# Decoder-style chain of FFN and mixer stages on one core: modulation weights scaled by ScalarE instead of GpSimd, with other loads, folds and score products re-ordered

## Chip, cores and metric

One core of one Trainium2 chip runs the whole program in one launch. The metric is the device time of that launch in microseconds (us). The kernel is written with raw engine programs: PE (TensorE, the matrix engine), ACT (ScalarE), DVE (VectorE), POOL (GpSimd) and SP (SyncE, which here issues the weight loads) each run their own list, and semaphores tie them together.

## What is computed

A batch of one, 256 tokens, width D = 1024, feed-forward width 2816, all in fp32. Two blocks follow each other. The first has two layers of FFN, mixer, FFN; its mixers are HGRN2 (a gated linear recurrence) and FOX (attention with forget gates). The second has FFN, a token mixer, FFN, each in a modulated frame whose shift, scale and gate come from one vector c.

```python
def first_block(x, ...):
    for layer in range(2):
        x = x + 0.5 * swiglu(rmsnorm(x, norm_g[layer, 0]), ffn_w_in[layer, 0], ffn_w_out[layer, 0])
        hn = rmsnorm(x, norm_g[layer, 1])
        x = x + (hgrn2_mixer(hn, ...) if layer == 0 else fox_mixer(hn, ...))
        x = x + 0.5 * swiglu(rmsnorm(x, norm_g[layer, 2]), ffn_w_in[layer, 1], ffn_w_out[layer, 1])
    return x

def second_block(x, c, w_ada, b_ada, ...):
    mod = (silu(c) @ w_ada + b_ada).reshape(1, 3, 3, 1024)      # w_ada: 1024 x 9216
    def sublayer(h, i, fn, resid_w):
        u = rms_norm(h, norm_pre[i]) * (1.0 + mod[:, i, 1]) + mod[:, i, 0]
        return h + resid_w * mod[:, i, 2] * rms_norm(fn(u), norm_post[i])
    # i = 0: swiglu (weight 0.5), i = 1: token_mixer (1.0), i = 2: swiglu (0.5)
```

## The kernel before, in words

**Stages.** `plan()` lists 13 stages: ffn, hg_in, hg_out, ffn, ffn, fox_in, fox_out, ffn, ffn, tm_in, branch, tm_out, ffn. The text calls the FFN stages by their norm number: 0, 2, 3, 5, 6 and 8. Every stage works on two tiles of 128 tokens.

**Products.** An fp32 product is made of three fp32r matmuls, hi·hi, hi·lo and lo·hi (`three`, lines 568 to 572; the names in a PE row with line 570, 571 or 572 tell which). So every weight exists twice: SP loads 1 MB (128 partitions x 2048 values, two DMAs of 512 KB) into one of four slots of `raw`; ACT's `split_hi` (line 1300) rounds the slot to `w_hi`; DVE's `split_lo` (line 1835) subtracts to make `w_lo`. The left operands are split in the same way (`actT_hi`, `hT_hi`, line 1417; `hT_lo`, line 1978).

**An FFN stage** has 11 chunks of 256 hidden columns (gate and up side by side). For chunk c PE runs `up(c,0)` and `up(c,1)`, 24 matmuls each with the weights of slots 0 and 1, and `down(c-1)`, 24 with those of slot 2. Between `up` and the next chunk stands the way of the hidden values: ACT's `silu` of the gate (lines 1420 to 1426), DVE's `product` with up (line 1988), `blocks`, a 32x32-block transposition (line 1973), ACT's `to_columns`, four DMAs that gather the blocks into columns (line 1411), the cast to `hT_hi` (`turned_hi`, line 1417) and DVE's `turned_lo` (line 1978). The last chunk uses slot 3 and a shorter way: PE transposes `hidden` itself (`turn_hidden_tile`, line 673), ACT writes the high part and DVE's `last_lo` the low. ACT's order within a chunk is: cast of slot 2, cast of hT, cast of slot 0, silu, cast of slot 1, `to_columns`. DVE's: w_lo of slot 2, hT_lo, w_lo of slot 0, product and transposition, w_lo of slot 1.

**Modulation.** silu(c) @ w_ada is not given to PE. POOL does it beside the FFN stages 2, 3, 5 and 6, in 72 units of 128 columns (`ada_unit`, lines 535 to 548), 18 per stage. A unit is a tile of 128 x 8 x 128 values (512 KB, loaded by POOL's own queue, line 533, into one of two buffers); POOL multiplies it with silu(c) (line 539) and adds the eight rows together in three steps (lines 542, 544, 548). Three units make a fold of 384 columns, which DVE finishes in `fold` (a transposition, line 1997, and a sum, line 2000). There are six folds in each of the four stages, placed after the chunks of the table `FOLD_AT`. The buffers lie in `arena`, one large array whose regions many stages share, so a row that says `arena<-arena` tells its operation by its line.

**Start.** ACT normalises x, turns it and casts slots 0 to 3; then it issues twenty small loads (norm vectors, c, biases, constants, the level masks) on its own queue before it enters the first FFN stage. `vectors()` uses them in chunk 5. `rounded_first` (lines 607 to 624) is PE's first product, one slot at a time; it waits for all of w_lo of slot 0 before its first matmul.

**HGRN.** The scores inside a chunk of tokens are made in eight levels (`score(n)`, line 831; `LEVELS`): level n covers the pairs that lie `LEVELS[n]` apart in a binary tree. Each is 16 matmuls of 128 columns by 64 (two tiles, eight heads; line 850), and DVE picks what belongs to the level with a predicated copy under a mask.

**FOX.** Four groups of four heads: `score(g)`, exponentials on ACT (line 1582), `turn_p(g)`, PE's transpositions of the weights (line 1008), and `weigh(g)`. Between them PE runs `unit(c,t)`, the products of the projection that are still due, as cover. DVE's `scaled(g)` inverts the sums and copies the result out, and `gated` multiplies it with the gate.

## Time and profile before

| | before |
|---|---|
| median of 3 runs | 1626.56 us (1624.83 to 1628.05) |
| the profiled execution | 1630.87 us, span 1629.1 us |
| mean granted TensorE clock | 0.995 of full |
| busy PE / PE weight loads | 98% / 81% of the span |
| busy DVE / ACT / POOL | 71% / 50% / 37% |
| moved by DMA | 337.23 MB, mean 207 GB/s |

A profile shows one execution, 4.3 us above the median of the three timed ones. The busy shares are averages over 13 stages. In the rows below, the idle time in brackets is that of the engine just before the row, with the instruction that released it.

### The profile page before, as it was taken

What the parts mean: (1) busy time and instruction counts of PE and PEld (TensorE: products, weight loads), DVE (VectorE), ACT (ScalarE), POOL (GpSimd) and SP (SyncE); (2) the same over time, 40 slices, a digit from 0 to 9 for tenths busy, and PEclk for the clock granted to TensorE, in tenths of its full rate; (3) what the DMA queues carried; (4) which work ended last, traced back from release to release, by engine and by line L of the source; (5) the groups of instructions that cost most, each with busy time, mean ns of one, the idle gap of its engine ahead of it and who ended that gap; (6) DMA issues with size and microseconds to landing.
All of it is one profiled execution on the core that took longest, in us unless ns stands there. A gap on an engine that the chain in (4) does not pass through costs nothing.

```text
span 1629.1 us, 20897 instructions
## 1 busy us (share of the span) xinstructions
PE 1590.8 (98%) x7517; PEld 1313.4 (81%) x7517; DVE 1152.6 (71%) x1114; ACT 821.4 (50%) x983; POOL 604.7 (37%) x368
## 2 busy tenths in 40 slices
PE   6999999999999999999999999999998999999998
PEld 5888888988888788877877888888886788878887
DVE  5565668777877787857777787688786557875554
ACT  5455563354445544445656444554435576564443
POOL 0000100068993599920008899079991000000000
PEclk9999999999999999999999999999999999999999
DMA  7767753348887688854437888758794444547672
GB/s 249 222 196 220 236 195 114 107 158 261 260 271 249 193 280 260 273 194 158 153 105 218 280 261 266 249 184 274 257 288 139 155 155 156 172 136 232 198 220 87
DMA packets 243133, 337.23 MB, mean 207 GB/s; under 512 B 14792, under 2 KB 180994, under 8 KB 243074
## 3 DMA queue, kind: packets, MB, share of 16 engines
q1 hardware_dynamic: 196256, 281.05, 52.6%
q0 software_dynamic: 10512, 38.54, 7.6%
q10 hardware_dynamic: 36306, 16.86, 4.1%
q8 instruction: 36, 0.59, 0.1%
q14 instruction: 23, 0.19, 0.0%
HBM read 319.62 MB, written 1.05 MB: 197 GB/s over the span
## 4 chain that ended last, share of the span: by engine, by line
PE 70%; POOL 17%; DVE 5%; ACT 3%; DMA 2%; issue 2%; ACTq 0%; SPq 0%; DVEq 0%; POOLq 0%
PE ps L570 20%; PE ps L572 20%; PE ps L571 20%; POOL arena L542 5%; POOL arena L539 4%; POOL arena L544 3%; POOL arena L548 2%; PE ps L616 2%; DVE w_lo L1835 2%; PE ps L850 2%; POOL arena L533 2%; DMA arena<-w_ada_dram 1%; PE ps L624 1%; PE ps L578 1%; ACT w_hi L1300 1%
## 5 line engine op out<-in xcount | busy, mean ns | idle before, releaser
L1835 DVE TENSOR_TENSOR w_lo<-raw,w_hi 128x2048 fp32r<-128x2048 f32 x266 | 683.6, 2581 | 204.5 <-ACT w_hi L1300 204.0
L1300 ACT CAST w_hi<-raw 128x2048 fp32r<-128x2048 f32 x266 | 505.7, 1911 | 308.7 <-PE ps L572 270.7
L570 PE MATMUL ps<-w_hi,actT_hi 128*128 128x512 f32 x1456 | 572.7, 393 | 6.4 <-DVE hidden L1988 2.9
L572 PE MATMUL ps<-w_hi,actT_lo 128*128 128x512 f32 x1456 | 567.6, 390 | 0.0
L571 PE MATMUL ps<-w_lo,actT_hi 128*128 128x512 f32 x1456 | 567.3, 390 | 0.0
L570 PEld LDWEIGHTS ps<-w_hi,actT_hi 128*128 128x128 f32 x1456 | 273.6, 188 | 66.5 <-issue 6.5
L572 PEld LDWEIGHTS ps<-w_hi,actT_lo 128*128 128x128 f32 x1456 | 273.7, 188 | 57.8
L571 PEld LDWEIGHTS ps<-w_lo,actT_hi 128*128 128x128 f32 x1456 | 273.9, 188 | 55.4
L542 POOL TENSOR_TENSOR arena<-arena 128x512 f32<-128x512 f32 x72 | 192.0, 2666 | 5.6
L570 PE MATMUL ps<-w_hi,hT_hi 128*128 128x512 f32 x480 | 189.6, 395 | 1.7 <-DVE hT_lo L1978 1.7
L539 POOL TENSOR_TENSOR arena<-arena,c_silu 128x1024 f32<-128x1024 f32 x72 | 153.1, 2126 | 95.6 <-DVE actT_lo L1863 44.6
L571 PE MATMUL ps<-w_lo,hT_hi 128*128 128x512 f32 x480 | 188.2, 392 | 0.0
L572 PE MATMUL ps<-w_hi,hT_lo 128*128 128x512 f32 x480 | 188.0, 392 | 0.0
L533 POOL DMA_DIRECT2D arena<-w_ada_dram x72 | 66.8, 928 | 308.4 <-PE ps L578 286.0
L1988 DVE TENSOR_TENSOR hidden<-gate,ps 128x256 f32<-128x256 f32 x132 | 77.0, 598 | 61.4 <-ACT gate L1426 50.8
L544 POOL TENSOR_TENSOR arena<-arena 128x256 f32<-128x256 f32 x72 | 107.0, 1487 | 5.7
L570 PEld LDWEIGHTS ps<-w_hi,hT_hi 128*128 128x128 f32 x480 | 91.1, 190 | 22.2 <-DVE hT_lo L1978 3.4
L572 PEld LDWEIGHTS ps<-w_hi,hT_lo 128*128 128x128 f32 x480 | 90.9, 189 | 19.4
L571 PEld LDWEIGHTS ps<-w_lo,hT_hi 128*128 128x128 f32 x480 | 91.1, 190 | 18.6
L1426 ACT ACTIVATE gate<-ps 128x256 f32<-128x256 f32 x66 | 25.3, 384 | 137.7 <-PE ps L572 120.4
L548 POOL TENSOR_TENSOR arena<-arena 128x128 f32<-128x128 f32 x72 | 80.4, 1116 | 14.8 <-DVE ada_fold L2000 9.3
L525 POOL CAST hidden<-arena 128x576 uint8<-128x576 f32 x1 | 2.8, 2782 | 191.6 <-PE ps L673 191.6
(257 smaller groups left out, 1349.9 us busy)
## 6 DMA issues: line engine op xcount, KB each, us to landing
raw<-ffn_w_in_dram SPq DMA_DIRECT2D x176, 512.0 KB, 4.9
raw<-ffn_w_out_dram SPq DMA_DIRECT2D x88, 512.0 KB, 4.4
arena<-w_ada_dram POOLq DMA_DIRECT2D x72, 512.0 KB, 6.3
raw<-ffn_w_gate_dram SPq DMA_DIRECT2D x44, 512.0 KB, 4.1
raw<-ffn_w_up_dram SPq DMA_DIRECT2D x44, 512.0 KB, 5.1
raw<-ffn_w_down_dram SPq DMA_DIRECT2D x44, 512.0 KB, 4.4
raw<-w_in_dram SPq DMA_DIRECT2D x40, 512.0 KB, 4.6
raw<-hg_w_in_dram SPq DMA_DIRECT2D x32, 512.0 KB, 4.9
```

What stands on the lines that cost most here:

```text
L533: nc.gpsimd.dma_start(ada_raw[:, n % 2, :, :], w_ada[:, :, n * ADA_U:(n + 1) * ADA_U]).then_inc(ada_loaded[n % 2], 16)
L539: nc.gpsimd.tensor_tensor(r, r, c_silu[:, :].unsqueeze(2).to_broadcast([P, KD, ADA_U]), ALU.mult)\
L542: nc.gpsimd.tensor_tensor(r[:, 0:4, :], r[:, 0:4, :], r[:, 4:8, :], ALU.add).then_inc(ada_by4, 1)
L544: nc.gpsimd.tensor_tensor(r[:, 0:2, :], r[:, 0:2, :], r[:, 2:4, :], ALU.add).then_inc(ada_by2, 1)
L548: nc.gpsimd.tensor_tensor(ada_acc[j % 2][:, at:at + ADA_U], r[:, 0, :], r[:, 1, :], ALU.add).then_inc(ada_summed, 1)
L570: nc.tensor.matmul(to, hi, whi, start=start, stop=False, skip_group_check=True)
L571: nc.tensor.matmul(to, hi, wlo, start=False, stop=False, skip_group_check=True)
L572: return nc.tensor.matmul(to, lo, whi, start=False, stop=stop, skip_group_check=True)
L616: nc.tensor.matmul(to, actT_hi[:, k, tok], half[:, s, w], start=k == 0 and half is w_hi, stop=False, skip_group_check=True)
L1300: nc.scalar.copy(w_hi[:, s, :], raw[:, s, :]).then_inc(hi_ready[s], 1)
L1835: nc.vector.tensor_tensor(w_lo[:, s, :], raw[:, s, :], w_hi[:, s, :].bitcast(F32), ALU.subtract)\
L1988: nc.vector.tensor_tensor(to, g, u, ALU.mult).then_inc(hidden_ready, 1)
```

## The change

Six things are changed. (1) The multiplication of the modulation's units goes from POOL to ACT: `ada_scale(n)` makes eight activations with silu(c) as a per-partition scale; chunk c of the stages 2, 3, 5 and 6 now carries two units, one between the casts of hT and slot 0, the other after `to_columns`. POOL keeps the three additions and the loads; there are three load buffers. (2) `FOLD_AT` has five chunks, and the sixth fold of a stage stands after the last product. (3) The twenty small loads are issued by POOL. (4) Slot 0 of the first stage is loaded, cast and subtracted in two halves, and PE waits for each half. (5) In HGRN the levels 32 and 64 are made as narrow products of 32x32 and 64x64, of which DVE copies all, with no mask. (6) In FOX, `turn_p(3)` moves into the middle of `unit(7,0)`, `scaled` is taken apart, and the gates of tile 0 are turned earlier.

The diff, its core:

```diff
-FOLD_AT = (2, 3, 5, 6, 8, 9)
+FOLD_AT = (2, 4, 5, 7, 8)
...
-        ada_raw = region(5120, 2, KD, ADA_U)
+        ada_raw = region(5120, 3, KD, ADA_U)
...
+                    if st.norm == 0 and half == 0 and isinstance(c, int) and c == 0:
+                        for part, done in ((slice(0, 2), front_loaded), (slice(2, 4), raw_loaded[0])):
+                            nc.sync.dma_start(to[:, part, 0:FC], w_gate[:, part, 0:FC]).then_inc(done, 16)
+                            nc.sync.dma_start(to[:, part, FC:COLS], w_up[:, part, 0:FC]).then_inc(done, 16)
+                        continue
...
+            pool.wait_ge(actT_ready, 4)
+
+            at = 48
+            for v, n in ((a["norm_pre_2"].rearrange("l i (k p) -> (l i k) p", p=P), 24),
+                         (a["norm_post_2"].rearrange("l i (k p) -> (l i k) p", p=P), 24),
...
+            nc.gpsimd.dma_start(rows_a[at:at + 1, :], a["da_subln_2"]).then_inc(rows_loaded, 16)
+            nc.gpsimd.dma_start(rows_b[0:72, :], a["b_ada_2"].rearrange("l (k p) -> (l k) p", p=P)).then_inc(rows_loaded, 16)
...
+            nc.gpsimd.dma_start(zf_raw[:, :, :], tiled(a["fox_w_in"][0])[:, :, 4 * D:FOX_IN]).then_inc(small_loaded, 16)
+            nc.gpsimd.dma_start(consts[:, P:], a["consts"][:, P:]).then_inc(consts_loaded, 16)
+            nc.gpsimd.dma_start(levels_raw, a["levels"]).then_inc(levels_loaded, 16)
+
...
             pool.wait_ge(hT_turned, 2)
             nc.gpsimd.tensor_copy(levels, levels_raw).then_inc(levels_ready, 1)
...
 
             pool.wait_ge(turned, 4 * (by_name["hg_out"].turned + 1))
             pool.wait_ge(c_ready, 1)
 
             def ada_load(n):
-                nc.gpsimd.dma_start(ada_raw[:, n % 2, :, :], w_ada[:, :, n * ADA_U:(n + 1) * ADA_U]).then_inc(ada_loaded[n % 2], 16)
+                nc.gpsimd.dma_start(ada_raw[:, n % 3, :, :], w_ada[:, :, n * ADA_U:(n + 1) * ADA_U]).then_inc(ada_loaded[n % 3], 16)
...
+                j, r = n // ADA_PER, ada_raw[:, n % 3, :, :]
                 at = (n % ADA_PER) * ADA_U
-                pool.wait_ge(ada_loaded[n % 2], 16 * (n // 2 + 1))
-                nc.gpsimd.tensor_tensor(r, r, c_silu[:, :].unsqueeze(2).to_broadcast([P, KD, ADA_U]), ALU.mult)\
-                    .then_inc(ada_scaled, 1)
                 pool.wait_ge(ada_scaled, n + 1)
-                nc.gpsimd.tensor_tensor(r[:, 0:4, :], r[:, 0:4, :], r[:, 4:8, :], ALU.add).then_inc(ada_by4, 1)
-                pool.wait_ge(ada_by4, n + 1)
-                nc.gpsimd.tensor_tensor(r[:, 0:2, :], r[:, 0:2, :], r[:, 2:4, :], ALU.add).then_inc(ada_by2, 1)
-                pool.wait_ge(ada_by2, n + 1)
+                nc.gpsimd.tensor_tensor(r[:, 0:4, :], r[:, 0:4, :], r[:, 4:8, :], ALU.add).then_inc(ada_halved, 1)
+                pool.wait_ge(ada_halved, 2 * n + 1)
+                nc.gpsimd.tensor_tensor(r[:, 0:2, :], r[:, 0:2, :], r[:, 2:4, :], ALU.add).then_inc(ada_halved, 1)
+                pool.wait_ge(ada_halved, 2 * n + 2)
                 if j >= 2 and n % ADA_PER == 0:
                     pool.wait_ge(ada_folded, j - 1)
                 nc.gpsimd.tensor_tensor(ada_acc[j % 2][:, at:at + ADA_U], r[:, 0, :], r[:, 1, :], ALU.add).then_inc(ada_summed, 1)
...
-                    if n == first + half // 2:
-                        pool.wait_ge(actT_ready, 4 * ((8 if first else 4) + 1))
+                    if n % (half // 2) == 0:
+                        pool.wait_ge(ada_scaled, n + 1)
+                        ada_load(n + 2)
                     ada_unit(n)
-                    if n + 2 < first + half:
-                        ada_load(n + 2)
+                    if n + 3 < first + half and n + 1 != first + half // 2:
+                        ada_load(n + 3)
...
                 tok = slice(t * P, (t + 1) * P)
                 for s in range(2):
                     pe.wait_ge(actT_hi_ready, 4 * st.turned + 2 * t + s + 1)
-                    pe.wait_ge(lo_ready[s], st.filled[s] + 1)
+                    if st.norm == s == t == 0:
+                        pe.wait_ge(front_lo, 1)
+                    else:
+                        pe.wait_ge(lo_ready[s], st.filled[s] + 1)
...
+                        if st.norm == s == t == 0 and kk == 2:
+                            pe.wait_ge(lo_ready[s], st.filled[s] + 1)
                         k, w = 4 * s + kk, slice(kk * COLS, (kk + 1) * COLS)
                         for half in (w_hi, w_lo):
                             nc.tensor.matmul(to, actT_hi[:, k, tok], half[:, s, w], start=k == 0 and half is w_hi, stop=False,
...
+                def narrow(n, t, h):
+
+                    size = LEVELS[n]
+                    beside = P // 2 // size
+                    for block in range(beside):
+                        rows = block * 2 * size + (h % 2) * size
+                        at = block * 2 * size
+                        to = ps[rows:rows + size, level_bank(n, t), (h // 2) * size:(h // 2 + 1) * size]
+                        last = nc.tensor.matmul(to, tile(hg_kT, t, h)[:, at:at + size], tile(hg_Q, t, h)[:, at + size:at + 2 * size],
+                                                start=True, stop=True, skip_group_check=True)
+                    return last
+
...
                                 rhs = tile(hg_qT, t, h)
+                            elif LEVELS[n] >= 32:
+                                last = narrow(n, t, h)
...
                 turn_p(2)
                 unit(6, 1)
                 weigh(2)
-                turn_p(3)
-                unit(7, 0)
...
             def token_mixer(st):
 
@@ -1378,6 +1427,13 @@
                 turn(nxt, 2)
...
 
+            def front():
+
+                act.wait_ge(front_loaded, 32)
+                nc.scalar.copy(w_hi[:, 0, 0:SLOT // 2], raw[:, 0, 0:SLOT // 2]).then_inc(front_hi, 1)
+                act.wait_ge(raw_loaded[0], 32)
...
+                        if t == b == 0 and st is None:
+                            front()
+                        elif t == 0:
                             split_hi(b, nxt.filled[b])
...
@@ -1429,13 +1487,23 @@
...
                 to_columns(0)
-                def middle(c):
+                def ada_scale(n):
+                    act.wait_ge(ada_loaded[n % 3], 16 * (n // 3 + 1))
+                    for k in range(KD):
+                        last = nc.scalar.activation(ada_raw[:, n % 3, k, :], ada_raw[:, n % 3, k, :], ACT.Copy, scale=c_silu[:, k:k + 1])
...
+
+                def middle(c, unit=None):
                     split_hi(2, filled[2] + c - 1)
                     turned_hi(c - 1)
+                    if unit is not None:
+                        ada_scale(unit)
                     split_hi(0, filled[0] + c)
                     silu(c)
                     split_hi(1, filled[1] + c + 1)
                     to_columns(c)
+                    if unit is not None:
+                        ada_scale(unit + 1)
...
+                elif st.norm in FOLD_IN:
+                    for c in range(1, NF - 1):
+                        middle(c, ADA_PER * FOLD_IN[st.norm] + 2 * (c - 1))
...
-
-            at = 48
-            for v, n in ((a["norm_pre_2"].rearrange("l i (k p) -> (l i k) p", p=P), 24),
-                         (a["norm_post_2"].rearrange("l i (k p) -> (l i k) p", p=P), 24),
-                         (a["c_2"].rearrange("b (k p) -> (b k) p", p=P), KD),
-                         (a["hg_lb_logits"].rearrange("l (k p) -> (l k) p", p=P), HG_H), (a["hg_out_norm_g"], 1)):
-                nc.scalar.dma_start(rows_a[at:at + n, :], v).then_inc(rows_loaded, 16)
...
-            nc.scalar.dma_start(zf_raw[:, :, :], tiled(a["fox_w_in"][0])[:, :, 4 * D:FOX_IN]).then_inc(zf_loaded, 16)
-            nc.scalar.dma_start(consts[:, P:], a["consts"][:, P:]).then_inc(consts_loaded, 16)
-            nc.scalar.dma_start(levels_raw, a["levels"]).then_inc(levels_loaded, 16)
...
+            def front():
+
+                for at, hi, lo in ((slice(0, SLOT // 2), front_hi, front_lo), (slice(SLOT // 2, SLOT), hi_ready[0], lo_ready[0])):
+                    dve.wait_ge(hi, 1)
+                    nc.vector.tensor_tensor(w_lo[:, 0, at], raw[:, 0, at], w_hi[:, 0, at].bitcast(F32), ALU.subtract)\
+                        .then_inc(lo, 1)
...
+                if st is None:
+                    front()
+                else:
+                    split_lo(0, nxt.filled[0])
...
                 product(NF - 1, False)
+                if st.norm in FOLD_IN:
+                    fold(FOLD_IN[st.norm] + len(FOLD_AT))
                 last_lo(st, 0)
...
@@ -2089,6 +2153,15 @@
                             to = hg_sc[:, t, :, :].rearrange("p g (n two h) -> p g n two h", two=2, h=h)[:, :, :, 1, :]
                             got = ps[:, level_bank(n, t), :].rearrange("p (g n h) -> p g n h", g=HG_H, h=h)
                             m_all = m.rearrange("p (n h) -> p n h", h=h).unsqueeze(1).to_broadcast([P, HG_H, P // (2 * h), h])
+                        if h >= 32:
+                            for odd in range(2):
+                                for block in range(P // 2 // h):
+                                    at, rows = 2 * h * block, 2 * h * block + h * odd
+                                    last = nc.vector.tensor_copy(hg_sc[at:at + h, t, odd:HG_H:2, at + h:at + 2 * h],
+                                                                 ps[rows:rows + h, level_bank(n, t), 0:HG_H // 2 * h]
+                                                                 .rearrange("p (g n) -> p g n", g=HG_H // 2))
+                            last.then_inc(hg_masked, 1)
+                            continue
                         nc.vector.copy_predicated(to, m_all, got).then_inc(hg_masked, 1)
...
-                def scaled(g):
...
                     rinv = f_rinv.rearrange("p (t g pair odd) -> p g t odd pair", t=2, g=4, odd=2)[:, g]
                     step(nc.vector.reciprocal(rinv, sums))
+
+                def keep_result(g):
...
                 dve.wait_ge(fx_o, 2)
                 step.wait()
                 for t in range(TILES):
                     step.mark(gated(0, t))
                 split_lo(0, nxt.filled[0])
+                inverse_sums(3)
+                gated(1, 0).then_inc(src_ready, 1)
+                keep_result(3)
+                dve.wait_ge(fx_o, 4)
+                turn_gated(0)
                 split_lo(1, nxt.filled[1])
-                scaled(3)
-                dve.wait_ge(fx_o, 4)
-                step.wait()
-                for t in range(TILES):
-                    gated(1, t).then_inc(src_ready, 1)
-                    if t == 0:
-                        turn_gated(0)
+                gated(1, 1).then_inc(src_ready, 1)
```

**ACT, inside the chunks of FFN stages 2, 3, 5 and 6.** Before, one chunk (line 1300 is the cast of a slot, 1417 that of hT, 1422 and 1426 the silu, 1411 `to_columns`):

```order
L1300 CAST w_hi<-raw 128x2048
L1414 ISA
L1417 CAST hT_hi<-arena 128x512
L1297 ISA
L1300 CAST w_hi<-raw 128x2048
L1421 REGISTER_ALU
L1422 ACTIVATE gate<-ps 128x256
L1425 REGISTER_ALU
L1426 ACTIVATE gate<-ps 128x256
L1297 ISA
L1300 CAST w_hi<-raw 128x2048
L1411 DMA arena<-arena 128x1x128 x4
```

Now, one chunk (1349 is the cast of a slot, 1475 that of hT, 1480 and 1484 the silu, 1469 `to_columns`, 1493 `ada_scale`):

```order
L1349 CAST w_hi<-raw 128x2048
L1475 CAST hT_hi<-arena 128x512
L1493 ACTIVATE arena<-arena,c_silu 128x128 x8
L1349 CAST w_hi<-raw 128x2048
L1480 ACTIVATE gate<-ps 128x256
L1484 ACTIVATE gate<-ps 128x256
L1349 CAST w_hi<-raw 128x2048
L1469 DMA arena<-arena 128x1x128 x4
L1493 ACTIVATE arena<-arena,c_silu 128x128 x8
```

The first unit stands ahead of the cast of slot 0, the second ahead of the next chunk's cast of slot 2.

**DVE, at the end of such a stage.** Before (1835 is w_lo, 1978 hT_lo, 1988 the product, 2042 `last_lo`, 1997 and 2000 the fold):

```order
L1835 TENSOR_TENSOR w_lo<-raw,w_hi 128x2048
L1997 STREAM_TRANSPOSE arena<-arena 128x384
L2000 TENSOR_REDUCE ada_fold<-arena 128x12
L1835 TENSOR_TENSOR w_lo<-raw,w_hi 128x2048
L1978 TENSOR_TENSOR hT_lo<-arena,hT_hi 128x512
L1835 TENSOR_TENSOR w_lo<-raw,w_hi 128x2048
L1988 TENSOR_TENSOR hidden<-gate,ps 128x256 x2
L2042 TENSOR_TENSOR hT_last_lo<-ps,hT_last_hi 128x256
```

Now (1887 is w_lo, 2040 hT_lo, 2050 the product, 2106 `last_lo`, 2059 and 2062 the fold):

```order
L1887 TENSOR_TENSOR w_lo<-raw,w_hi 128x2048 x2
L2040 TENSOR_TENSOR hT_lo<-arena,hT_hi 128x512
L1887 TENSOR_TENSOR w_lo<-raw,w_hi 128x2048
L2050 TENSOR_TENSOR hidden<-gate,ps 128x256 x2
L2059 STREAM_TRANSPOSE arena<-arena 128x384
L2062 TENSOR_REDUCE ada_fold<-arena 128x12
L2106 TENSOR_TENSOR hT_last_lo<-ps,hT_last_hi 128x256
```

The fold stood two w_lo ahead of the last product; it stands behind the product now, ahead of `last_lo`.

## Rows read from the trace of the kernel before

**Rows 1.** The page: busy time, share of the span and instructions of each engine.
```profile
PE 1590.8 (98%) x7517; PEld 1313.4 (81%) x7517; DVE 1152.6 (71%) x1114; ACT 821.4 (50%) x983; POOL 604.7 (37%) x368
```
**Rows 2.** Timeline, first stage: start, duration, engine, line, operation, [idle before <-releaser].
```profile
12.10 0.77 PE L616 MATMUL ps<-w_hi,actT_hi 128*128 128x512 f32 x1 [2.73 <-DVE w_lo L1835]
12.90 2.28 DVE L1835 TENSOR_TENSOR w_lo<-raw,w_hi 128x2048 fp32r<-128x2048 f32 x1
...
26.75 1.28 ACT L1422 ACT_TABLE_LOAD   x1 [5.23 <-issue]
29.22 0.47 PE L570 MATMUL ps<-w_hi,actT_hi 128*128 128x512 f32 x1 [2.94 <-DVE hidden L1988]
```
**Rows 3.** Timeline, ends of stages 3 and 6; last row: stage 2, chunk 1.
```profile
705.83 0.58 DVE L1997 STREAM_TRANSPOSE arena<-arena 128x384 f32<-128x384 f32 x1 [8.18 <-POOL arena L548]
712.60 0.66 PE L673 MATMUL ps<-consts_sb,hidden 128*128 128x128 f32 x2 [3.24 <-DVE hidden L1988]
...
1226.51 0.58 DVE L1997 STREAM_TRANSPOSE arena<-arena 128x384 f32<-128x384 f32 x1 [8.38 <-POOL arena L548]
1233.28 0.66 PE L673 MATMUL ps<-consts_sb,hidden 128*128 128x128 f32 x2 [4.84 <-DVE hidden L1988]
...
556.70 0.50 PE L570 MATMUL ps<-w_hi,actT_hi 128*128 128x512 f32 x1 [1.69 <-DVE w_lo L1835]
```
**Rows 4.** Windows: PE, PEld, DVE, ACT, POOL busy us; clock, DMA share, GB/s.
```profile
30.40:33.80 3.40, 3.40 (x10) 2.68 (x9) 2.29 (x1) 0.10 (x1) 0.00 (x0) 0.57 0.22 48
713.10:716.50 3.40, 3.40 (x10) 2.65 (x10) 2.80 (x3) 3.18 (x3) 0.00 (x0) 0.58 1.00 352
1231.90:1238.70 6.80, 5.42 (x16) 4.37 (x17) 5.88 (x6) 3.66 (x4) 0.00 (x0) 0.53 0.87 305
```
**Rows 5.** Timeline, PE in the FOX mixer: `turn_p(3)`.
```profile
832.51 0.66 PE L1008 MATMUL ps<-consts_sb,arena 128*128 128x128 f32 x4 [1.81 <-ACT arena L1582]
```
**Rows 6.** Timeline, POOL: multiplication and first addition of one modulation unit.
```profile
857.95 1.89 POOL L539 TENSOR_TENSOR arena<-arena,c_silu 128x1024 f32<-128x1024 f32 x1 [3.10 <-DMA arena<-w_ada_dram]
859.92 1.29 POOL L542 TENSOR_TENSOR arena<-arena 128x512 f32<-128x512 f32 x1
```
**Rows 7.** Timeline, ACT: eight activations from PSUM (`turn`), one from SBUF (`exps`).
```profile
542.62 2.18 ACT L1319 ACTIVATE actT_hi<-ps,cols 128x128 fp32r<-128x128 f32 x8 [0.40 <-PE ps L578]
...
829.24 0.39 ACT L1582 ACTIVATE arena<-arena,small 128x128 f32<-128x128 f32 x1
```
**Rows 8.** Timeline, stage 2, DVE and ACT through one chunk; last row: next silu.
```profile
608.03 4.40 DVE L1835 TENSOR_TENSOR w_lo<-raw,w_hi 128x2048 fp32r<-128x2048 f32 x1 [1.23 <-ACT w_hi L1300]
608.76 0.38 ACT L1422 ACTIVATE gate<-ps 128x256 f32<-128x256 f32 x1 [0.75 <-PE ps L572]
...
611.76 1.91 ACT L1300 CAST w_hi<-raw 128x2048 fp32r<-128x2048 f32 x1
612.35 1.16 DVE L1988 TENSOR_TENSOR hidden<-gate,ps 128x256 f32<-128x256 f32 x2
613.55 0.71 DVE L1973 STREAM_TRANSPOSE arena<-hidden 128x512 f32<-128x512 f32 x1
614.29 2.52 ACTq L1411 DMA_DIRECT2D arena<-arena  x4
...
625.08 0.39 ACT L1422 ACTIVATE gate<-ps 128x256 f32<-128x256 f32 x1 [0.75 <-PE ps L572]
```
**Rows 9.** Timeline, stage 2: PE begins `up(1,0)`; ACT casts hT of chunk 0.
```profile
549.41 0.39 PE L570 MATMUL ps<-w_hi,actT_hi 128*128 128x512 f32 x1
...
557.32 0.62 ACT L1417 CAST hT_hi<-arena 128x512 fp32r<-128x512 f32 x1 [1.16 <-DMA arena<-arena]
```
**Rows 10.** Timeline: a level's 32 score products; eight narrow products; DVE in HGRN.
```profile
304.68 3.68 PE L850 MATMUL ps<-arena 128*128 128x64 f32 x32
...
1275.64 0.28 PE L789 MATMUL ps<-ada_fold,lb 128*32 128x24 f32 x8
...
313.00 1.23 DVE L2143 COPY arena<-ps 128x1024 f32<-128x1024 f32 x1 [2.65 <-PE ps L858]
```

More of the change, by code:

```diff
@@ L1056, in fox, with turn_gates @@
                 weigh(2)
[L1057 to L1058 removed]
+                unit(7, 0, lambda: turn_p(3))
                 weigh(3)
[L1060 removed]
+                def turn_gates():
+                    pe.wait_ge(fx_o, 4)
+                    turn_tile(by_name["fox_out"], fx_g, 0)
+                unit(7, 1, turn_gates)
             def token_mixer(st):
```

58 lines of the change are left out of this document (32 added, 26 removed).

## The prediction

> **What bounds the kernel now.** I read the page's busy times first: the matrix engine (PE) is busy 1590.8 of 1629.1 us [rows 1], so only its waits and its slow stretches can be won. I then went along PE's timeline for every place where it stood still, and asked the rows before it who was late. The reader should see four kinds of place.
>
> At the start, the first product (12.10) waits for w_lo of slot 0, and the up product of chunk 1 (29.22) waits 2.94 us, because ScalarE (ACT) began its silu table load only at 26.75, after 5.23 us of issuing loads [rows 2]. In the two later modulation stages PE waits 3.24 us (712.60) and 4.84 us (1233.28) for `hidden`; just before, VectorE (DVE) had stood 8.18 and 8.38 us in `fold`, waiting for GpSimd (POOL) [rows 3]. At 556.70 PE waits 1.69 us for a w_lo that POOL had held up. Behind the three long stalls PE's granted clock is at its lower level (1.2 GHz instead of 2.4): windows of 3.4, 3.4 and 6.8 us read 0.57, 0.58 and 0.53 [rows 4]. Half speed costs half of each: 1.7, 1.7 and 3.4 us. Last, the FOX mixer's `turn_p(3)` waits 1.81 us for the exponentials [rows 5].
>
> **The change, part by part.** The sum is made against the profiled execution (1630.87 us, span 1629.1).
>
> *Head.* PE's 12.10 is set by w_lo of the whole slot. With half slots it can start when actT_hi is there, about 1.3 us sooner. But eight products at the slow pitch later it needs w_lo of slot 1, which ends at 15.18 [rows 2] and moves by some 0.3 us only. I count 0.5 us. The twenty small loads leave ACT's queue: the table load comes 5.2 us sooner, so the 2.94 us go, and with them the slow window behind. Sum: -0.5 - 2.9 - 1.7 = **-5.1 us**. POOL issues those loads instead; it was idle, and PE needs the vectors first in chunk 5, five chunks of 16 us later, so I cost this at nothing. If that cover failed, the wait would sit in `turn_vectors`.
>
> *Old modulation stalls.* DVE's two long folds and the contested w_lo go: -(3.24 + 1.7) - (4.84 + 3.4) - 1.69 = **-14.9 us**. POOL's multiplication of 1.89 us per unit goes too; what remains begins with an addition of 1.29 us [rows 6]. POOL is then paced by ACT, two units per chunk.
>
> *New ACT work.* Each chunk gets two units of eight 128x128 activations with a per-partition scale. No row shows that form from SBUF. The nearest: eight such from PSUM take 2.18 us, and one from SBUF with a per-partition bias 0.39 us [rows 7], so eight with no overlap would be 3.1. I take 2.3, near the overlapped row, since ACT's neighbours overlap by about 0.1 us wherever they are queued. A ScalarE page of the Trainium skill ("ScalarE: Activation LUTs", section "What ACT_TABLE_LOAD costs") speaks against the change here: with one pointer operand it gives 280 ns + 0.833 ns per element and an overlap of 93 ns, an estimate of 2.44 us for eight. By it the sum below would be some 6 us higher; the PSUM row is the only measured one, and no run here shows the SBUF form yet.
>
> What is queued behind those units matters more than ACT's load. Follow one chunk round [rows 8]: DVE's transposition of `hidden` 0.71, four DMA issues on ACT 2.52 and a pause of about 0.3, unit B 2.3, cast of slot 2 1.91, cast of hT 0.62, unit A 2.3, cast of slot 0 1.91, w_lo of slot 0 2.29, the two products of `hidden` 1.16, and again the transposition. That is 16.0 us, less some 0.4 for ACT's overlaps, plus what POOL takes from DVE: a w_lo of 2.29 became 4.40 beside POOL, and unit A's additions start just before w_lo of slot 0, so 0.2 to 1.0. The loop is 15.8 to 16.6 us long; PE's chunk is 16.32 (silu to silu, 608.76 to 625.08). So ACT has no time left to catch up.
>
> And it starts late. In chunk 1 the cast of hT ends 8.5 us after PE begins `up(1,0)` (557.94 against 549.41) [rows 9]. Unit A, cast, w_lo, products and transposition put the transposition's end at 8.5 + 2.2 + 1.8 + 2.5 + 1.9 = 16.9, which is 6 us after the end of `up(1,1)` (10.9), where it was 2.8 before. If the loop holds this, the last unit B ends about 10.8 us after `up(9,1)`. Then cast 1.9, w_lo of slot 2 2.3, turned_lo 0.6, w_lo of slot 3 2.3 and the first product 0.6 come one after another, with some port wait: 18.7, while PE wants `hidden` at 16.3. **Each of the four stages ends in a stall of about 2.4 us**, of the same kind as at 712.60, plus about 0.3 in chunk 1 and 0.3 in the others: 4 x 3.0 = **+12.0 us**. A stall of 2.94 us cost a slow window, one of 1.69 none; I give two of the four one: **+3.4 us**. The fold that moves to the stage's end (1.15 us) stands behind the product there and ahead of last_lo, which PE wants 2.7 us later; I cost it at nothing.
>
> *FOX.* `turn_p(3)` moves into the middle of unit (7,0), 2.7 us of matmuls later, and the 1.81 us vanish; 1.5 net, since the transposes lose their clean cover: **-1.5 us**. The reordered gates wait for nothing that is late.
>
> *HGRN scores.* The levels 32 and 64 took 3.68 us of PE each by the row, the last one's tail of some 0.2 included: 32 instructions, 0.11 apart. Now 64 instructions of 32x32 and 32 of 64x64. Eight of 32x24 took 0.28 us, so 0.035 each is the low end, and 0.115 the high [rows 10]: 96 of them between 3.4 and 11.0 us against 7.0, that is from -3.6 to +4.0. I take 0.045 and 0.08 (the smaller form lies near the 32x24 row): 5.5 against 7.0, **-1.5 us**. DVE's eight plus four small copies instead of four predicated ones lengthen it by about a microsecond; it waited 2.65 us for PE just after.
>
> Sum: -5.1 - 14.9 + 12.0 + 3.4 - 1.5 - 1.5 = -7.6, so 1623.3 for that execution. It lay 4.3 us above the median of the runs shown; the forecast against the median is **1619 us**.
>
> **The rivals.** *The loop has room.* If a unit takes about 2.1 us, or POOL rarely meets w_lo of slot 0, the loop is 15.8 and gains half a microsecond per chunk: after nine chunks the 3 us of delay are gone and a stage loses 1.0, with no slow window. -5.1 - 14.9 - 3.0 (FOX and HGRN) + 4.0 = -19.0, that is **1607.6**. For it: eight from PSUM take 2.18. Against it: the late start of the loop, and that the row from SBUF reads 0.39 us for one.
>
> *The loop sets the pace (slower).* In ACT's chain between units B and A, from a unit length of about 2.5 us on, the loop exceeds 16.32 by more than 0.3 and each chunk pays. At 2.7 us and a port wait of 1.0 it is 17.1: 9 x 0.8 + 2.6 + 1.7 = 11.5 per stage, +46 in all against the 23.0 removed elsewhere: +23, about **1649**; at 2.55 us about 6.5 per stage, +26, that is 1630. Against it: 2.7 needs activations that hardly overlap.
>
> *The narrow scores cost.* If small matmuls keep the pitch of 0.11, the change there is +4.0 instead of -1.5: **1624.5**. For it: the pitch was the same for 64 and 128 columns. Against it: the 32x24 row.
>
> *The head gains nothing*, because slot loads become the limit once PE is 5 us earlier: 1624. ACT's casts of those slots were held up by its own issues, not by a load, so I hold it unlikely.
>
> **How the numbers follow.** About 0.2% (3.3 us) is what a measurement of this kernel can tell from no change: faster is under 1623.3, slower over 1629.8. Forecast 0.45, room in the loop 0.30, pace set by the loop 0.13, narrow scores or head failing 0.12. Most of the first and all of the second are faster: 0.72. The upper edge of the first and the last make 0.15 the same, the third 0.13 slower. The range reaches to the second (1606) and into the third (1632).
>
> **What would show it.** PE's waits: none at 29 us; no long fold waits on DVE; at each of the four stages' ends a PE wait of about 2.4 us for `hidden`, with DVE running two w_lo ahead of the product. ACT: eight activations in about 2.3 us, and its cast of slot 2 beginning 10 us after `up` ends, not 5.4. If those stalls are missing, the first rival holds; if PE waits in every chunk for w_lo of slot 2 or `hidden`, the second; if the narrow scores' instructions read above 0.075 us on average, the third. The forecast is wrong if ACT's chain is not what DVE waits for at the stage's end.

## The result and the profile after

The changed kernel takes 1632.83 us (median of 20 runs, 1626.28 to 1637.47), the kernel before 1626.43 (20 runs, 1622.86 to 1628.83). The ratio is 1.0035, 95% interval 1.0023 to 1.0047 (the two medians alone give 1.0039): **slower by 0.35%**, where 1619 was forecast, so faster, with a range up to 1632. The execution profiled after took 1634.08 us, 3.2 more than the one before; their difference stage by stage is the first thing to read. I took the start of each stage from PE's timeline (its first transposition of an activation tile) and compared the lengths; the bracket joins the four stages that carry the modulation, for which the forecast was one sum.

| part | before, us | change, us | forecast |
|---|---|---|---|
| start and FFN 0 | 191.73 | -2.97 | -5.1 |
| HGRN | 127.70 | -3.50 | -1.5 |
| FFN 2 | 187.45 | +6.93 | } |
| FFN 3 | 189.21 | -3.65 | } together |
| FFN 5 | 187.57 | +11.25 | } +0.5 |
| FFN 6 | 196.22 | -2.97 | } |
| FOX | 119.37 | -1.80 | -1.5 |
| all else | | below 0.1 | 0 |

So the loss is in the four stages with the modulation: +11.56 in sum against +0.5. The page's busy times, the line that answers to [rows 1]:

```profile
PE 1592.0 (98%) x7549; PEld 1308.3 (80%) x7549; DVE 1064.2 (65%) x1123; ACT 978.5 (60%) x1560; POOL 399.7 (24%) x315
```

ACT gained 157 us of work, POOL and DVE lost 205 and 88; PE's time is the same. No engine beside PE is busy for more than 65% of the span, and yet the kernel is slower. PE's waits, from its timeline at the ends of stages 2, 3, 5 and 6, with one from the middle of stage 5 (to set beside [rows 3]):

```profile
522.67 0.66 PE L704 MATMUL ps<-consts_sb,hidden 128*128 128x128 f32 x2 [3.73 <-DVE hidden L2050]
710.94 0.41 PE L704 MATMUL ps<-consts_sb,hidden 128*128 128x128 f32 x2 [2.81 <-DVE hidden L2050]
973.53 0.50 PE L596 MATMUL ps<-w_hi,hT_hi 128*128 128x512 f32 x1 [0.58 <-DVE hT_lo L2040]
1045.87 0.66 PE L704 MATMUL ps<-consts_sb,hidden 128*128 128x128 f32 x2 [4.79 <-DVE hidden L2050]
1237.18 0.41 PE L704 MATMUL ps<-consts_sb,hidden 128*128 128x128 f32 x2 [2.28 <-DVE hidden L2050]
```

Each of the four stages ends in the wait that was forecast, for the `hidden` that was forecast, but they sum to 13.6 us and not 9.6. In the middle of stage 5 stand seven waits of 0.20 to 0.58 us, for hT_lo and for `hidden`, where the kernel before has none of the kind. Behind three of the four the clock is low (windows; the columns are those of [rows 4]):

```profile
521.70:528.50 6.80, 5.83 (x16) 4.60 (x17) 6.73 (x8) 4.17 (x6) 0.00 (x0) 0.50 0.48 154
713.50:715.10 1.60, 1.60 (x10) 1.29 (x9) 1.60 (x2) 1.56 (x3) 0.00 (x0) 1.00 0.91 350
1044.00:1050.80 6.80, 4.93 (x13) 3.99 (x14) 6.73 (x8) 5.08 (x6) 0.00 (x0) 0.50 0.49 155
1237.70:1242.80 5.10, 5.10 (x18) 3.95 (x17) 5.03 (x5) 3.58 (x4) 0.00 (x0) 0.67 1.04 390
```

The column behind the five engines is the granted clock: 0.50 is half speed, and 0.67 says that a part of that window ran at half speed. Half of 5.83 and of 4.93, and a third of 5.10 us, are 7.1 us lost to half speed, where I had 3.4.

Now one round of stage 5, from one transposition of `hidden` to the next, 16.99 us later; PE's chunk is 16.32. These are rows of the timelines of DVE, ACT and POOL, to set beside [rows 8]:

```profile
945.15 0.71 DVE L2035 STREAM_TRANSPOSE arena<-hidden 128x512 f32<-128x512 f32 x1
945.52 0.90 POOL L561 DMA_DIRECT2D arena<-w_ada_dram  x1 [0.30 <-POOL arena L573]
945.89 2.54 ACTq L1469 DMA_DIRECT2D arena<-arena  x4
948.48 2.45 ACT L1493 ACTIVATE arena<-arena,c_silu 128x128 f32<-128x128 f32 x8 [4.86 <-issue]
950.84 1.90 ACT L1349 CAST w_hi<-raw 128x2048 fp32r<-128x2048 f32 x1
953.55 0.62 ACT L1475 CAST hT_hi<-arena 128x512 fp32r<-128x512 f32 x1 [0.81 <-DMA arena<-arena]
954.08 2.45 ACT L1493 ACTIVATE arena<-arena,c_silu 128x128 f32<-128x128 f32 x8
956.43 1.90 ACT L1349 CAST w_hi<-raw 128x2048 fp32r<-128x2048 f32 x1
958.36 2.71 DVE L1887 TENSOR_TENSOR w_lo<-raw,w_hi 128x2048 fp32r<-128x2048 f32 x1 [2.21 <-ACT w_hi L1349]
960.99 1.11 DVE L2050 TENSOR_TENSOR hidden<-gate,ps 128x256 f32<-128x256 f32 x2
962.14 0.71 DVE L2035 STREAM_TRANSPOSE arena<-hidden 128x512 f32<-128x512 f32 x1
```

The chain is the one that the prediction followed, with one link that it had as a pause of 0.3: at 952.74 ACT is done with the cast of slot 2 and stands still for 0.81 us until the four gathers of `to_columns` have landed. (A DMA has landed when it signals that it is done; its issue alone takes 0.6 us.) And POOL, whose additions of the first unit have just ended, issues its next load of 512 KB at 945.52, ahead of the gathers at 945.89. In the rows of the page that count DMA issues (KB each, median us to landing) the gathers read, after:

```profile
arena<-arena ACTq DMA_DIRECT2D x240, 64.0 KB, 5.0
```

and before:

```profile
arena<-arena ACTq DMA_DIRECT2D x240, 64.0 KB, 3.7
```

These rows count all six FFN stages. In the four with the modulation alone, the medians are 5.5 after and 4.25 before.

Mean length of rounds 2 to 9 in the four stages: 16.60, 16.49, 17.14 and 16.72 us. When the cast of hT waits for nothing, it begins 7.5 us after the transposition and the round is 16.2 to 16.5 (8 of the 32 rounds); else it begins at 7.7 to 9.5, at worst 10.6, and the round is up to 19.0. The wait for the gathers is 0.47, 0.57, 0.91 and 0.60 us per round in the mean of each stage. When POOL issues its load plays a part already here: in 11 of the 32 rounds the load goes out some 0.45 us ahead of the transposition, and 8 of these casts wait for nothing; in the other 21 it goes out later, between 0.04 us ahead of it and 0.9 us behind it, and every one of these casts waits.

### The profile page after: what moved, and what is told of

The parts are those of the page before. It is cut to its first block, busy times and chain, and to the rows that moved or that the text cites. A ratio compares the mean times of both kernels' runs of the same rounds, so it can differ in the third digit from the quotient of the medians.

```text
span 1632.3 us, 21153 instructions
## 1 busy us (share of the span) xinstructions
PE 1592.0 (98%) x7549; PEld 1308.3 (80%) x7549; DVE 1064.2 (65%) x1123; ACT 978.5 (60%) x1560; POOL 399.7 (24%) x315
## 4 chain that ended last, share of the span: by engine, by line
PE 54%; ACT 15%; DMA 10%; DVE 9%; issue 7%; ACTq 5%; SPq 0%; DVEq 0%
PE ps L596 14%; PE ps L598 14%; PE ps L597 14%; DMA arena<-arena 9%; ACT arena L1493 7%; ACT w_hi L1349 6%; ACTq L1469 5%; PE ps L647 4%; DVE w_lo L1887 3%; DVE hidden L2050 3%; PE ps L655 2%; DVE arena L2035 2%; PE ps L896 1%; PE ps L604 1%; DMA raw<-ffn_w_in_dram 0%
## 5 line engine op out<-in xcount | busy, mean ns | idle before, releaser
L1887 DVE TENSOR_TENSOR w_lo<-raw,w_hi 128x2048 fp32r<-128x2048 f32 x265 | 621.9, 2357 | 348.8 <-ACT w_hi L1349 348.5
L596 PE MATMUL ps<-w_hi,actT_hi 128*128 128x512 f32 x1456 | 572.2, 393 | 2.4 <-DVE w_lo L1887 0.7
L1493 ACT ACTIVATE arena<-arena,c_silu 128x128 f32<-128x128 f32 x576 | 176.5, 389 | 171.9 <-issue 171.9
L567 POOL TENSOR_TENSOR arena<-arena 128x512 f32<-128x512 f32 x72 | 93.5, 1299 | 185.7 <-ACT arena L1493 185.0
L573 POOL TENSOR_TENSOR arena<-arena 128x128 f32<-128x128 f32 x72 | 131.8, 1831 | 5.7
L569 POOL TENSOR_TENSOR arena<-arena 128x256 f32<-128x256 f32 x72 | 94.5, 1312 | 5.6
L647 PE MATMUL ps<-w_hi,actT_hi 128*128 128x512 f32 x144 | 59.3, 412 | 2.8 <-DVE w_lo L1887 1.4
```

The source lines that it names most:

```text
L567: nc.gpsimd.tensor_tensor(r[:, 0:4, :], r[:, 0:4, :], r[:, 4:8, :], ALU.add).then_inc(ada_halved, 1)
L569: nc.gpsimd.tensor_tensor(r[:, 0:2, :], r[:, 0:2, :], r[:, 2:4, :], ALU.add).then_inc(ada_halved, 1)
L573: nc.gpsimd.tensor_tensor(ada_acc[j % 2][:, at:at + ADA_U], r[:, 0, :], r[:, 1, :], ALU.add).then_inc(ada_summed, 1)
L596: nc.tensor.matmul(to, hi, whi, start=start, stop=False, skip_group_check=True)
L647: nc.tensor.matmul(to, actT_hi[:, k, tok], half[:, s, w], start=k == 0 and half is w_hi, stop=False, skip_group_check=True)
L1493: last = nc.scalar.activation(ada_raw[:, n % 3, k, :], ada_raw[:, n % 3, k, :], ACT.Copy, scale=c_silu[:, k:k + 1])
```

## The experiments

Two theories stood at first. *ACT's row* (that of the prediction): the round is the sum of ACT's work on the chain, and both units count alike. *Landing*: the gathers' landing sets the cast of hT, so that only the first unit counts, and what delays the landing is the trouble. A rival to both: the loss is in the other parts of the change, or in their being together.

**e1: everything but the scaling.** The changed kernel with `ada_load`, `ada_unit`, ACT's `middle`, `FOLD_AT` and the place of the sixth fold as before. The core of the edit:

```diff
-                    if unit is not None:
-                        ada_scale(unit)
...
-FOLD_AT = (2, 4, 5, 7, 8)
+FOLD_AT = (2, 3, 5, 6, 8, 9)
```

> The changed kernel with the modulation as before: POOL multiplies, two buffers, six folds inside the loop, no unit on ACT. Kept: small loads on POOL, half slots, narrow scores, FOX order. If the parts add up as the two traces have them (head -3.1, HGRN -3.5, FOX -1.8, the two output stages -1.1 us), it takes 9.5 us less than the kernel before: 1617. If instead the loss of the change sits in one of these four parts, or they don't add, it lies within 3 us of the kernel before.

Measured 1619.18 us, ratio 0.9962 [0.9948, 0.9975]. The four other parts are worth 7 us; the scaling turns this into a loss. The 1617 was 2 us too good.

**e2 and e3: one unit cut down to one activation.**

```diff
-                    for k in range(KD):
+                    for k in range(KD - 1 if n % 2 == 0 else 0, KD):
```

This is e2, the first unit; e3 has `n % 2 == 1`, the second. Both leave seven of that unit's eight rows unscaled.

> The changed kernel, but the first unit of each chunk (between the casts of hT and slot 0) does one of its eight activations, so half of the modulation's rows stay unscaled. Theory landing (the round of a chunk goes transposition, four issues, landing of hT at 8.0 to 8.6 us, cast of hT, first unit, cast of slot 0, w_lo, product): the round falls from 16.2 to 17.0 us by 2.1, below PE's 16.32, and the stalls of all four stages go: 1632.8 - 27 = 1606. Theory of the prediction (ACT's own row of work is the round, both units count alike): the same, 1606. If neither unit matters (POOL's additions or the loads do it): 1630.

> The changed kernel, but the second unit of each chunk (behind to_columns) does one of its eight activations. Theory landing: hT lands at 8.0 to 8.6 us whether or not ACT is busy in between, so the cast of hT keeps its place, the round stays near 16.3 to 16.9 us, and the time stays above 1622. Theory of the prediction: the second unit is a term of the round like the first, the round falls by 2.1, 1606.

e2: 1607.18, ratio 0.9878 [0.9863, 0.9893]. e3: 1608.01, ratio 0.989 [0.9873, 0.9907]. By the times, landing is refuted: the second unit is worth as much as the first. By the traces it isn't. In e3 ACT is free 2 us sooner, and then waits for the gathers 1.6 us longer (2.23 us per round in the mean, against 0.64). ACT's timeline, stage 5:

```profile
939.70 0.62 ACT L1475 CAST hT_hi<-arena 128x512 fp32r<-128x512 f32 x1 [1.68 <-DMA arena<-arena]
```

The cast of hT begins 7.3 us after the transposition there. The median of the 32 rounds is 7.6 us, against 8.3 with the whole unit, and the mean round is 16.25 instead of 16.74. Half a microsecond for 2 us of work taken out: so the landing does hold most of it back. But 16.25 lies below PE's 16.32 and 16.74 above, and with that half microsecond 25 us of the time are gone. My error in this expectation was to take a round that hardly changes for a time that hardly changes. In e2, too, the round fell by 0.5 and not by 2.1 (mean 16.21): w_lo of slot 0 now runs beside POOL's first addition and the start of its second, and takes 4.2 us in this round, 4.0 in the median instead of 2.6 (timelines of DVE and POOL):

```profile
991.66 4.20 DVE L1887 TENSOR_TENSOR w_lo<-raw,w_hi 128x2048 fp32r<-128x2048 f32 x1
992.39 1.30 POOL L567 TENSOR_TENSOR arena<-arena 128x512 f32<-128x512 f32 x1
993.77 2.68 POOL L569 TENSOR_TENSOR arena<-arena 128x256 f32<-128x256 f32 x1
```

**e4: the first unit elsewhere.** All work is done.

```diff
                     turned_hi(c - 1)
-                    if unit is not None:
-                        ada_scale(unit)
                     split_hi(0, filled[0] + c)
                     silu(c)
                     split_hi(1, filled[1] + c + 1)
+                    if unit is not None:
+                        ada_scale(unit)
                     to_columns(c)
```

> The changed kernel with the first unit moved from behind the cast of hT to behind the cast of slot 1, ahead of to_columns, where ACT waits some 2.3 us for DVE's transposition. All work is done. Both theories of the round: the unit leaves it, the round is some 14.5 us, stalls at the four stage ends go, 1606 to 1610. Rival: the unit ends later than the transposition, to_columns comes later by up to 2 us and hT with it; then the stalls stay and the time is 1625 or more.

Measured **1604.73 us** (1604.01 to 1605.31), ratio 0.9868 [0.9853, 0.9883]: faster than both kernels, by 1.3% than the one before. None of the four stage ends has a wait for `hidden` any more, and the rounds read 16.3, PE's own chunk, not the chain's 14.5: a chain shorter than the chunk waits for PE. ACT's timeline shows why the rival failed:

```profile
912.07 0.55 ACTq L1469 DMA_DIRECT2D arena<-arena  x1
912.33 0.69 ACT L1493 ACTIVATE arena<-arena,c_silu 128x128 f32<-128x128 f32 x2
912.65 0.63 ACTq L1469 DMA_DIRECT2D arena<-arena  x1
912.92 0.68 ACT L1493 ACTIVATE arena<-arena,c_silu 128x128 f32<-128x128 f32 x2
...
913.97 0.64 ACTq L1469 DMA_DIRECT2D arena<-arena  x1
914.09 3.02 ACT L1493 ACTIVATE arena<-arena,c_silu 128x128 f32<-128x128 f32 x10
917.02 1.90 ACT L1349 CAST w_hi<-raw 128x2048 fp32r<-128x2048 f32 x1
918.82 0.61 ACT L1475 CAST hT_hi<-arena 128x512 fp32r<-128x512 f32 x1
```

The unit stands ahead of the four issues in the program, and runs beside them: ACT computes while its queue issues. So both units together end 5.7 us after the transposition (911.33), just as one did behind the issues. The loads have moved as well, away from the gathers, whose median is 3.7 us again (4.0 in the four stages). So e4 changes two things at once, the unit's place and the moment of the loads, and doesn't tell their shares.

**e5 and e6: a dose less and a dose more.** e5 does six of the first unit's eight activations (it reads 1.87 instead of 2.45 us); e6 makes two of its rows in halves, ten activations (2.82 us).

```diff
-                    for k in range(KD):
+                    for k in range(0 if n % 2 else 2, KD):
```

That is e5; e6 is:

```diff
+                    r, half_row = ada_raw[:, n % 3, :, :], ADA_U // 2
                     for k in range(KD):
...
+                        for cols in ((slice(0, half_row), slice(half_row, ADA_U)) if n % 2 == 0 and k < 2 else (slice(0, ADA_U),)):
+                            last = nc.scalar.activation(r[:, k, cols], r[:, k, cols], ACT.Copy, scale=c_silu[:, k:k + 1])
```

> The changed kernel, but the first unit of each chunk does six of its eight activations (two rows stay unscaled). One takes about 0.29 us, so the round is 0.58 shorter. Theory threshold: only the part of a round above PE's 16.32 costs time. The rounds of the four stages read 16.60, 16.50, 17.14 and 16.72 in the changed kernel, an excess of 0.28, 0.18, 0.82 and 0.40 over eight rounds each: 13.4 us. The shorter round takes nearly all of it and some of the slow clock behind: 1632.8 - 13.4 - 5 = 1614. Rival, proportional: seven activations less gave 25.6, so two give 7: 1625.

> The changed kernel, but the first unit of each chunk is made of ten activations, two rows being scaled in halves of 64 columns: the same work, 0.4 to 0.5 us longer. Threshold: every stage is above 16.32 already, so all of it is paid, 8 rounds x 4 stages x 0.45 = 14, for 1645 to 1649. Rival: ACT waits for the landing of hT in any case and takes this up: 1633.

e5: 1619.39, ratio 0.9945 [0.9927, 0.9964]. e6: 1636.89, ratio 1.0062 [1.0041, 1.0082]. Both signs are as expected, and both sizes are less: -13.4 instead of -19, +4.1 instead of +12 to +16. The rounds tell why: their mean moved by -0.22 for -0.58, and by +0.20 for +0.37. In e5 the cast of hT waits 0.83 us in the mean instead of 0.64, and w_lo of slot 0 has a median of 2.7 us instead of 2.6. So what I had expected, that every microsecond above the threshold is paid in full, is wrong: four to five tenths of what was taken or given show in the round.

**e7: small loads.** It leaves seven eighths of the modulation's weights unread; the rest of the work stays.

```diff
-                nc.gpsimd.dma_start(ada_raw[:, n % 3, :, :], w_ada[:, :, n * ADA_U:(n + 1) * ADA_U])
+                nc.gpsimd.dma_start(ada_raw[:, n % 3, 0:1, :], w_ada[:, 0:1, n * ADA_U:(n + 1) * ADA_U])
```

> The changed kernel, but POOL loads an eighth of each modulation unit (64 KB instead of 512), so most of the scaled values are stale. If hT lands late (8.0 to 8.6 us after the transposition) because its four gathers share the DMA engines with these loads, it lands by about 7 us, the second unit and the cast of slot 2 end at 7.5 and set the round instead: about 16.2 us, and the time 1608 to 1615. If the landing is bound by the gathers themselves or by SP's weight loads, it stays at 8.0 to 8.6 and the time within 4 us of 1633.

Measured 1605.43, ratio 0.9867 [0.9842, 0.9892], better than its own expectation. ACT's timeline of one round, transposition at 914.34:

```profile
917.65 2.46 ACT L1493 ACTIVATE arena<-arena,c_silu 128x128 f32<-128x128 f32 x8 [3.51 <-issue]
920.01 1.89 ACT L1349 CAST w_hi<-raw 128x2048 fp32r<-128x2048 f32 x1
921.81 0.61 ACT L1475 CAST hT_hi<-arena 128x512 fp32r<-128x512 f32 x1
922.33 2.45 ACT L1493 ACTIVATE arena<-arena,c_silu 128x128 f32<-128x128 f32 x8
```

With the same work on ACT, DVE and POOL, the cast of hT never waits (it begins 7.5 us after the transposition in 35 of the 36 rounds, and at 7.7 in one). While the chain is what holds, the round is 15.84 to 15.92 us. The gathers' median is 3.3 (3.5 in the four stages). So this run shows that the modulation's loads are what makes the gathers late. It shows one thing more. The first round still ends late: the transposition of chunk 1 ends 4.0 to 4.7 us after PE's `up(1,1)`, much as in the changed kernel (4.4 to 5.1). But each round then gains some 0.46 us, until the transposition ends 1.83 us after `up`, and no stage ends in a wait.

**e8 to e11: the parts alone, on the kernel before.** e8 has the small loads on POOL and slot 0 in halves, e9 the scaling, e10 the narrow scores, e11 the FOX order. Each is its own hunks of the diff above.

> The kernel before with the two changes at the start alone: small loads issued by POOL, slot 0 in halves. In the traces the first stage ended 3.0 to 5.5 us sooner with them (2.97 in the changed kernel's profile, 3.58, 3.26, 5.47 and 4.42 in the four variants'). 1626.3 - 4.0 = 1622.3. If it were nothing but a shift of waits within the stage: 1626.

> The kernel before with the modulation's part of the change alone (scaling on ACT, two units per chunk, three buffers, folds). The four stages lost 6.9, 11.3 and won 3.7, 3.0 us in the changed kernel's profile, 11.6 in sum. If the parts add: 1626.4 + 11.6 = 1638. If the loss needs the other parts beside it (an earlier start of the chunks, loads on POOL's queue), 1630 or less.

> The kernel before with the narrow scores alone. By the traces the HGRN stage ends 3.5 us sooner: 1623. If DVE's twelve copies made something later outside that stage: 1626.

> The kernel before with the FOX order alone. By the traces that stage ends 1.8 us sooner: 1624.6. If turn_p(3) merely handed its wait to the next product: 1626.4.

| run | us | ratio, interval |
|---|---|---|
| e8, start | 1621.55 | 0.997 [0.9953, 0.9988] |
| e9, scaling | 1646.91 | 1.0131 [1.0113, 1.015] |
| e10, narrow scores | 1623.88 | 0.9984 [0.997, 0.9998] |
| e11, FOX | 1624.54 | 0.9987 [0.9966, 1.0008] |

e8 as expected. e9 is 20 us slower and not 12: its rounds are like those of the whole change or longer (means 17.03, 16.76, 16.79, 16.71), and it ends its stages in waits of 4.88, 2.22, 4.58 and 2.36 us. The four differences (-5.2, +20.0, -3.0, -2.4) sum to 9.4 where the whole has 6.4, so they add only roughly. For e10 and e11 the traces are sharper than the times: in e10 HGRN is 2.37 us shorter and FOX the same (3.50 in the changed kernel; e10's profile has 3.4 us at half clock there, from 300.39 on, which that one has not), in e11 FOX is 1.84 us shorter and HGRN the same. By the times alone e11 can't be told from no change.

**e12: the loads at another moment.** All work and ACT's order are those of the changed kernel.

```diff
-                    if n + 3 < first + half and n + 1 != first + half // 2:
-                        ada_load(n + 3)
+                    for m in (n + 2, n + 3) if n % 2 else ():
+                        if m < first + half and m != first + half // 2 + 2:
+                            ada_load(m)
```

> The changed kernel, all its work and ACT's order kept, but POOL issues both loads of a chunk behind the second unit's additions, about 11 us after the transposition begins, instead of one there and one 0.2 to 0.4 us after it, just ahead of the four gathers. Theory collision: hT lands late because that load's 512 KB go ahead of the gathers; then the gathers' median falls from 5.0 to about 3.7 us, hT is cast at 7.5 us, the rounds fall to some 15.9 and the time to 1606 to 1612. Rival, volume: any two loads per chunk delay the gathers alike; the rounds stay above 16.4 and the time at 1630.

Measured 1619.7, ratio 0.9957 [0.9943, 0.9971]: 13 us faster than the changed kernel, though not the 1606 to 1612 expected. The gathers' median did fall to 3.7 us over all six FFN stages, but in the four with the modulation only from 5.5 to 4.7. ACT's cast of hT waits for nothing in 19 of the 32 rounds, and most of these are then 15.86 long. This shows that the moment of the loads matters, not their volume alone. But ten of the 32 rounds are still 17.1 to 17.5. In nine of these hT is somewhat late again (7.9 to 9.3 us), and in nine w_lo of slot 0 takes 2.8 to 3.8 us instead of 2.5. The late gathers go with the same collision, from its other end: a load is now issued 11 to 12 us after a transposition and takes 7.3 us, so it can still be under way when the next one's gathers go out. Of the 36 rounds from the second of each stage on, the 13 in which the last of these loads has landed by 2.8 us after the transposition have gathers of 3.2 to 4.1 us (median of the four), and the 23 in which it lands later have 4.7 to 6.3. Which share of the missing 10 us belongs to the gathers and which to w_lo was not tried.

The rounds of all these runs beside the time of the execution in which they were read:

| | mean round, us | that execution, us |
|---|---|---|
| e7, small loads | 16.00 | 1606.2 |
| e2, first unit cut | 16.21 | 1610.0 |
| e3, second unit cut | 16.25 | 1605.7 |
| e4, first unit late | 16.27 | 1604.5 |
| e12, loads apart | 16.37 | 1614.7 |
| e5, two less | 16.52 | 1623.0 |
| the changed kernel | 16.74 | 1634.1 |
| e6, two halved | 16.94 | 1637.6 |

Below 16.3 the time is flat within 6 us; from there to the changed kernel's 16.74 it climbs by 30. That agrees with a threshold at PE's chunk of 16.32. It isn't sharp, for the round is not all that counts: e2 (16.21) still ends two of its stages in waits of 2.16 and 1.88 us and e3 (16.25) three of them in waits of 0.84 to 1.22, where their chain starts some 4 to 5 us late and hardly gains; e4 (16.27) starts 2.0 to 2.4 us late, for its first unit is no longer in that way, and has no wait at all.

## Why the prediction was wrong

**The chain was right.** Transposition, issues, second unit, cast of slot 2, cast of hT, first unit, cast of slot 0, w_lo, products: this is what the round consists of, the late start of the loop is there (4.4 to 5.1 us after `up(1,1)`, where 6 were forecast), and PE's waits stand where they were put. With the gathers out of the way (e7) the round is 15.86, inside the 15.8 to 16.6 forecast. But that the loop would hold its delay doesn't follow from such a round: in e7 it makes the delay good, no stage ends in a wait, and the time is 1605.4. That is the first rival, "the loop has room" (15.8, 1607.6), at a unit of 2.45 us and not of 2.1. So the stalls came where they were forecast, but for another reason than the one given.

**The step that failed** is the term "four DMA issues on ACT 2.52 and a pause of about 0.3", with the cast of hT simply following that of slot 2. The gathers' landing was left out as a second way round the same place; ACT's wait for it, put at nothing, measured 0.5 to 0.9 us per round in the stages' means. The row that should have warned was among those shown: in [rows 9] ACT waits 1.16 us for the gathers. The round in the kernel before could bear this, since ACT waited again right behind the cast of hT, for PE, in 24 of 32 rounds for 1.4 us or more (kernel before, ACT's timeline, in the round of [rows 8]):

```profile
619.72 0.62 ACT L1417 CAST hT_hi<-arena 128x512 fp32r<-128x512 f32 x1 [0.57 <-DMA arena<-arena]
622.41 1.92 ACT L1300 CAST w_hi<-raw 128x2048 fp32r<-128x2048 f32 x1 [2.07 <-PE ps L572]
```

The change puts 2.45 us into that place, and sends POOL's load at the very moment of the gathers. The prediction had asked what queues behind ACT's instructions and not what queues behind, or beside, its DMAs. The mean rounds of 16.49 to 17.14 us are 0.6 to 1.3 longer than the 15.86 of e7. The Trainium skill ("DMA: Bandwidth & Descriptors", section "Issuing engines are not separate DMA queues") says that transfers from SP, ACT and POOL run on the same 16 engines and interleave; the medians of 5.0 and 3.3 us agree.

**The unit** took 2.45 us and not 2.3. The page of the Trainium skill that the prediction cites ("ScalarE: Activation LUTs", section "What ACT_TABLE_LOAD costs") gave an estimate of 2.44, and the trace agrees with it; I chose the row from PSUM over it. Two units in a round make 0.3 us of it, as much as lay between the 16.0 of the sum and PE's 16.32.

**The old stalls** were counted at 14.9 us, and then the 4.3 us by which the profiled execution exceeded the median were taken off as well. This counts the excess twice. In e10 and e11, where nothing of the modulation was changed, stage 3 is 4.4 and 4.8 us shorter than in the profile of before: the excess lay in the wait and the slow window at 712.60 [rows 3, 4], which are in the 14.9. That wait comes in some executions and not in others: in e8, also with the old modulation, it is 2.62 us, and that profile lies 3.2 us above its own median. The forecast from this working should have been 1623.3. And the slow window at the end of stage 6 was counted at 3.4 us, half of its 6.83, though PE was busy for only 4.95 us of it, which makes 2.5; with that, 1624.2.

**The balance**, execution against execution: forecast -7.6, measured +3.2. The four stages are 11.1 us worse than forecast: 4.0 of it in the waits at the ends, 3.7 in the slow clock. The remaining 3.4 are made of several things: the waits within the stages are 4.4 us where 2.4 were forecast, the old slow window gave 0.9 less than counted, short waits of before that nobody had counted took 2.5 with them, and PE's busy time grew by 2.8 beyond what the slow clock explains, the cause of which is open. The start is 2.1 worse, HGRN 2.0 and FOX 0.3 better.

**The start.** The silu's table load no longer waits and PE's 2.94 us are gone, as said. The products of slot 1 wait 1.45 us instead, as the prediction half saw:

```profile
15.64 0.77 PE L647 MATMUL ps<-w_hi,actT_hi 128*128 128x512 f32 x1 [1.45 <-DVE w_lo L1887]
```

What the two changes gain at the start ran from -2.54 (e5) to -5.47 us (e3) between profiles. In the one shown here PE's starts are still 0.43 us apart until 19.2; in e8, where the stage is 5.4 us shorter, 0.23 from 15.3 on.

**HGRN** was worth 3.5 us, since the narrow products are far quicker than I had them: 0.014 us for the small form, below my lower bound of 0.035, and 0.037 for the larger, where I took 0.08 (compare [rows 10]; PE's timeline):

```profile
295.34 0.46 PE L870 MATMUL ps<-arena 128*32 128x32 f32 x32
296.79 0.46 PE L870 MATMUL ps<-arena 128*32 128x32 f32 x32 [1.00 <-DVE arena L2136]
300.12 1.17 PE L870 MATMUL ps<-arena 128*64 128x64 f32 x32
```

**FOX** is right, at 1.80 for 1.5. **The rivals:** the slower one, "the loop sets the pace" (1630 to 1649), is what happened, with the mechanism half right: it was given a unit of 2.55 or 2.7 us as its condition, and came about at 2.45 through the landing. A chance of 0.13 was too low for a loop that the prediction itself had put within half a microsecond of its limit.

## What to carry to other kernels

When a chain of several engines is within a few per cent of the pace of the engine it feeds, the price of a new piece of work is less its length than on which side of that pace the round ends, and how late the chain starts; here 0.5 us in a round of 16.7 went with some 25 us of the time. Every DMA on such a chain is a second way round: take its landing from the trace, in the stages that matter and with its worst cases, and ask which transfers the change sends at the same moment. And before a difference between the profiled execution and the median is carried over, look whether it lies in what the change removes.

## What had not been expected of the hardware

ACT computes while its queue issues DMAs, if the computation stands first: eight activations and four issues took about 2.6 us together in e4, 5.0 one after the other in the changed kernel. Thirty-two instructions of the 32x32 products took 0.46 us, 0.014 each, against 0.115 for those of 128 by 64 [rows 10]. And w_lo, 2.29 us alone, took up to 4.2 beside POOL's additions, 2.6 in the median of the changed kernel and 4.0 in that of e2, so that work taken from ACT came back on DVE.
